# Two decoder layers on one core: the product a @ w_out of both MLPs as Strassen's seven block products

## What is computed

```python
def _mlp(h, w_in, w_out):
    a = jnp.square(jax.nn.relu(h @ w_in))     # h: 512 x 1024, w_in: 1024 x 4096
    return a @ w_out                          # w_out: 4096 x 1024

for l in range(DEPTH):                        # DEPTH = 2
    h = _rmsnorm(x, norm_mix[l])
    x = x + (_pool_mixer(...) if l < N_A else _diff_attn(...))
    x = x + _mlp(_rmsnorm(x, norm_mlp[l]), w_mlp_in[l], w_mlp_out[l])
    if l == N_A - 1:                          # after layer 0: shared keys and values
        kv = _rmsnorm(x, kv_norm) @ w_kv
```

## Time and profile before

| | |
|---|---|
| median of 3 runs | 1009.54 us (1009.34 to 1012.75) |
| the profiled execution's own time | 1010.91 us |
| its span, first to last instruction | 1009.1 us |
| PE busy (matmuls) | 990.1 us, 98% |
| DVE, ACT, POOL busy | 517.5, 407.1, 58.3 us |
| HBM read | 92.56 MB |
| MLP of layer 0, of layer 1 | about 32 to 385 us, about 652 to 1005 us |

### The profile page before, as it was taken

The page is one execution under the profiler, slowest core; times in us unless marked ns, Lnnn a source line. Parts: engine busy times, 40 slices in busy tenths (PEclk is TensorE's granted clock), DMA queues, the critical chain, the costliest instruction groups (busy, mean ns, idle before and its releaser), DMA issues.

```text
span 1009.1 us, 12484 instructions
## 1 busy us (share of the span) xinstructions
PE 990.1 (98%) x4663; PEld 816.4 (81%) x4663; DVE 517.5 (51%) x815; ACT 407.1 (40%) x586; POOL 58.3 (6%) x44
## 2 busy tenths in 40 slices
PE   8999999999999999899999999999999999999998
PEld 6888888888888887678888877888888888888886
DVE  5855422144442427888888885755441234444221
ACT  8643421223341315566666673534331113342110
POOL 2100000000000000222222230000000000000000
PEclk9999999999999999899999998999999999999999
DMA  7423223223323222232332222223323222423231
GB/s 241 121 84 108 100 85 124 84 83 91 117 83 119 91 62 63 66 90 84 85 86 86 73 83 84 84 84 91 116 84 123 87 84 87 121 83 105 83 105 42
DMA packets 82300, 95.15 MB, mean 94 GB/s; under 512 B 2690, under 2 KB 61107, under 8 KB 82267
## 3 DMA queue, kind: packets, MB, share of 16 engines
q1 hardware_dynamic: 80954, 89.95, 28.8%
q0 software_dynamic: 1312, 4.74, 1.6%
HBM read 92.56 MB, written 4.74 MB: 96 GB/s over the span
## 4 chain that ended last, share of the span: by engine, by line
PE 92%; DVE 4%; issue 1%; ACT 1%; DMA 1%; SPq 0%; DVEq 0%
PE bank L1087 29%; PE bank L1089 29%; PE bank L1088 29%; PE bank L1261 2%; PE bank L1271 1%; PE bank L1299 1%; PE bank L1216 1%; DMA work<-in_x_dram 1%; DVE work L914 1%; DVE neg_max L950 1%; DVE work L946 0%; PE bank L1185 0%; ACT work L635 0%; DVE a_low_buf L732 0%; DVE xT L830 0%
## 5 line engine op out<-in xcount | busy, mean ns | idle before, releaser
L723 DVE TENSOR_TENSOR w_low<-raw,w_high 128x2048 fp32r<-128x2048 f32 (+1 forms) x75 | 163.3, 2177 | 233.8 <-ACT w_high L463 233.7
L1087 PE MATMUL bank<-h_high_buf,w_high 128*128 128x512 f32 x640 | 252.9, 395 | 0.0
L1089 PE MATMUL bank<-h_high_buf,w_low 128*128 128x512 f32 x640 | 250.1, 391 | 0.0
L1088 PE MATMUL bank<-h_low_buf,w_high 128*128 128x512 f32 x640 | 249.9, 390 | 0.0
L463 ACT ACTIVATE w_high<-raw 128x2048 fp32r<-128x2048 f32 (+1 forms) x77 | 140.1, 1819 | 254.7 <-PE bank L1089 254.7
L1087 PE MATMUL bank<-a_high_buf,w_high 128*128 128x512 f32 x528 | 208.0, 394 | 4.1 <-DVE a_low_buf L732 4.0
L1089 PE MATMUL bank<-a_high_buf,w_low 128*128 128x512 f32 x528 | 206.6, 391 | 0.0
L1088 PE MATMUL bank<-a_low_buf,w_high 128*128 128x512 f32 x528 | 206.5, 391 | 0.0
L1087 PEld LDWEIGHTS bank<-h_high_buf,w_high 128*128 128x128 f32 x640 | 120.8, 189 | 27.4 <-issue 2.5
L1089 PEld LDWEIGHTS bank<-h_high_buf,w_low 128*128 128x128 f32 x640 | 120.6, 188 | 25.6
L1088 PEld LDWEIGHTS bank<-h_low_buf,w_high 128*128 128x128 f32 x640 | 120.8, 189 | 24.3
(11 more groups left out here) (133 smaller groups left out, 821.2 us busy)
## 6 DMA issues: line engine op xcount, KB each, us to landing
raw<-in_w_mlp_in_dram SPq DMA_DIRECT2D x32, 1024.0 KB, 5.5
raw<-in_w_mlp_out_dram SPq DMA_DIRECT2D x32, 1024.0 KB, 5.0
raw<-in_w_kv_dram SPq DMA_DIRECT2D x16, 512.0 KB, 4.0
raw<-in_w_q_dram SPq DMA_DIRECT2D x8, 512.0 KB, 5.3
raw<-in_w_o_dram SPq DMA_DIRECT2D x3, 1024.0 KB, 4.9
bias_by_distance<-bias_rows_by_distance POOLq DMA_DIRECT2D x8, 320.0 KB, 4.1
work<-in_x_dram SPq DMA_DIRECT2D x4, 512.0 KB, 5.1
work<-bias_by_distance POOLq DMA_DIRECT2D x8, 256.0 KB, 3.0
```

The costliest lines, as they stand in the source:

```text
L723: dve.tensor_tensor(w_low_buf[s][:, 0:cols], raw[s][:, 0:cols], f32(w_high_buf[s][:, 0:cols]), ALU.subtract)\
L1087: pe.matmul(acc, w_hi, m_hi, start=start, stop=False)
L1088: pe.matmul(acc, w_hi, m_lo, start=False, stop=False)
L1089: return pe.matmul(acc, w_lo, m_hi, start=False, stop=stop)
```

## The change

`a @ w_out` is computed per quarter of the 4096 rows of `w_out` (four pairs of chunks). In a quarter, `a` is split in two by tokens (2 x 256) and in two by rows, and `w_out` in two by rows and in two by columns (2 x 512). Seven products of blocks replace eight. Per pair of chunks ACT squares into a buffer `pre`, DVE forms four sums of blocks there (S1 to S4), and high and low parts of seven operands of 256 columns are made in one instruction each. A quarter's seven units follow in the order P1, P5, P2, P6, P3, P7, P4, each behind the fourth pair of its quarter and, but for the last quarter, behind the first pair of the next. A unit in layer 0 is 48 matmuls on 256 columns (weights: blocks of w_out), in layer 1 24 matmuls on 512 columns (weights: tokens). DVE adds or subtracts the product banks to the stream (`take`), 16 times a quarter; c21 is a second use of the banks of P7.

The sums of w_out blocks are made in `raw` buffers, of which there are four in the MLPs: T1 = B11 + B12 and T3 = B12 + B22 by a plain load and an adding transfer that POOL starts, T2 = T1 + B22 by DVE, T4 = T2 + B21 by an adding transfer. All loops of the MLPs are written out. The parts of the diff below are POOL's adding transfers, ACT's `split_out` and the end of its loop over the pairs (n = 2 to 15), DVE's `out_quarter`, and PE's `out_product`. The residual's transposes in layer 1 move behind the third and fourth pair. The inputs of the keys are prepared in the order of chunks 4 to 7, 0 to 3.

```diff
+            def add_blocks(l):
...
+                for q in range(NQ):
+                    pool.wait_ge(w_landed[0], landed[l, q, "t1"])
+                    pool.dma_start(tile3(mlp_raw[l][0], NPAIR), w_out_block(l, q, 0, 1), accum_op=ALU.add).then_inc(t1_landed, 16)
+                    pool.wait_ge(w_landed[1], landed[l, q, "t3"])
+                    pool.dma_start(tile3(mlp_raw[l][1], NPAIR), w_out_block(l, q, 1, 1), accum_op=ALU.add).then_inc(t3_landed, 16)
+                    pool.wait_ge(w_low, u_out(l, q, P6) + 1)
+                    pool.dma_start(tile3(mlp_raw[l][0], NPAIR), w_out_block(l, q, 1, 0), accum_op=ALU.add).then_inc(t4_landed, 16)
...
+            def split_out(l, q, p):
...
+                if p == P5:
+                    act.wait_ge(t1_landed, 16 * n)
+                elif p == P6:
+                    act.wait_ge(t2_ready, n)
+                elif p == P7:
+                    act.wait_ge(t3_landed, 16 * n)
+                elif p == P4:
+                    act.wait_ge(t4_landed, 16 * n)
+                else:
+                    act.wait_ge(w_landed[OUT_RAW[p]], landed[u])
+                act.wait_ge(w_used, u - 1)
+                act.activation(w_high_buf[u % 2][:, :], mlp_raw[l][OUT_RAW[p]], ACT.Copy).then_inc(w_high, 1)
...
+                    operands_high(l, n - 1)
...
+                    squares(l, n, 0)
...
+                    squares(l, n, 1)
+                    if n % 4 == 0:
+                        out_quarter(l, n // NPAIR - 1)
...
+            def out_quarter(l, q):
...
+                if q == NQ - 1:
+                    operand_sums(l, N_IN - 1)
+                split_out(l, q, P5)
+                if q == NQ - 1:
+                    operands_low(l, N_IN - 1, A12)
+                take_1(l, q, 0)
+                add_t2(l, q)
+                split_out(l, q, P2)
+                take_1(l, q, 1)
+                take_5(l, q, 0)
+                take_5(l, q, 1)
+                split_out(l, q, P6)
+                take_2(l, q, 0)
+                take_2(l, q, 1)
+                split_out(l, q, P3)
...
+                split_out(l, q, P4)
+                take_7(l, q, 0)
+                take_7(l, q, 1)
+                if q < NQ - 1:
+                    split_in(l, 4 * q + 5)
+                take_c21(l, q, 0)
+                take_c21(l, q, 1)
+                if l == 0 and q == NQ - 1:
+                    split_low(U_HEAD, 1)
+                    prep_kv(range(2))
+                take_4(l, q, 0)
+                if l == 0 and q == NQ - 1:
+                    prep_kv(range(2, 4))
+                take_4(l, q, 1)
...
+            def out_product(l, q, p, acc, fresh):
...
+                        if l == 0:
+                            for m in range(2):
+                                last = product(acc[t][:, m * TH:(m + 1) * TH], *column(u % 2, k * S + (2 * t + m) * P), a_hi, a_lo,
+                                               start and m == 0, stop and m == 1, not fresh)
                         else:
+                            tile, w = slice(t * P, (t + 1) * P), slice(k * S, (k + 1) * S)
+                            last = product(acc[t][:, :], a_hi[:, tile], a_lo[:, tile], w_high_buf[u % 2][:, w], w_low_buf[u % 2][:, w],
+                                           start, stop, not fresh)
```

More of the change, by code:

```diff
@@ L486, in norm_root_step, with prep_x @@
                    .then_inc(norm_rooted, 1)
-            def prep_x(h_base, x_base, dst, gain, chunks=range(KC)):
+            def prep_x(x_base, dst, gain, chunks=range(KC)):
                 for c in chunks:
@@ L491, in prep_x @@
                     input_high(dst[:, c, :], xT[:, c, :], params[:, gain + c:gain + c + 1])
[L493 to L504, removed]
@@ new lines, in squares, with operand_high @@
+            def squares(l, n, j):
+                cc = 2 * (N_IN * l + n) + j
+                if j == 0 and n >= 2:
+                    act.wait_ge(a_low, a_count(l, n - 2))
+                act.wait_ge(z_taken, cc + 1)
+                b = pre[n % 2]
+                act.activation(b[:, 0:8:7, :] if j == 0 else b[:, A12:A22 + 1, :], relu_buf[j].rearrange("p (h n) -> p h n", h=2), ACT.Square)\
+                   .then_inc(z_squared, 1)
+            def operand_high(l, n, first, last):
+                if n >= NPAIR:
+                    act.wait_ge(w_used, u_out(l, n // NPAIR - 1, P4) + 1)
+                act.activation(operand(a_high_flat, n, first, last), pre[n % 2][:, first:last, :].rearrange("p s n -> p (s n)"), ACT.Copy)\
+                   .then_inc(a_high, 1)
@@ L694, in _ @@
             o_high(6)
[L695 removed]
+            split_wo(U_WO + 2)
             o_copies(H - 1)
@@ new lines, in block, with take @@
+            def block(l, row, col, t):
+                if l == 0:
+                    return xT[:, 4 * col + 2 * t:4 * col + 2 * t + 2, row * TH:(row + 1) * TH]
+                return out_sb[:, 2 * row + t, col * S:(col + 1) * S]
+            def take(l, q, p, t, acc, row, col, op):
+                count = taken(l, q, p, t)
+                if t == 0:
+                    dve.wait_ge(tile_done, 7 * (NQ * l + q) + (P7 if p == "c21" else p) + 1)
+                else:
+                    dve.wait_ge(w_used, u_out(l, q, P7 if p == "c21" else p) + 1)
+                if count > 2:
+                    dve.wait_ge(tile_taken, count - 2)
+                x = block(l, row, col, t)
+                src = acc[t][:, :].rearrange("p (m n) -> p m n", m=2) if l == 0 else acc[t][:, :]
+                dve.tensor_tensor(x, x, src, op).then_inc(tile_taken, 1)
```

595 lines of the change are left out of this document (358 added, 237 removed).

## The result

| | before | after |
|---|---|---|
| median | 1010.75 us (4 runs) | 985.04 us (4 runs, 983.86 to 985.32) |
| span of the profiled execution | 1009.1 | 983.0 |
| its own time | 1010.91 | 984.77 |
| matmuls on PE | 4663 | 5143 |

The ratio is 0.9742 (0.972 to 0.9764). In a later series the changed kernel took 983.41 us (five runs) and the kernel before 1009.48 (nine), a ratio of 0.9742 (0.9721 to 0.9762). The forecast was 979.2, with 972 to 995 as its range; the first series misses it by 5.8 us and the later one by 4.2.

What follows compares the result with a forecast made beforehand. PE's back-to-back matmuls were taken to bound the kernel. Matmuls -38.7, waits +4.4 and transition +4.0 sum to -30.3 us: 1010.9 to 980.6 for the profiled execution, so a median of 979.2 us, range 972 to 995.

Steps and rivals of the forecast that it cites:

- 1344 x 0.117 = 157.2 us, so -16.9: Layer 0's w_out on PE: 1344 matmuls on 256 columns at 0.117 us each, against 174.1 us before.
- Layer 1's -21.8: Layer 1's w_out on PE: 672 instead of 768 matmuls on 512 columns, 152.3 us against 174.1.
- P5 and P2: PE's waits in w_out: P5 1.8 us in all, P2 in each layer's last quarter 2.6; sum +4.4 us.
- the covers that the forecast named: In the MLPs, transfers, takes and preparation beside the w_in pairs were to be hidden behind PE's work, at no cost.
- The transition: From layer 0 to the heads: low parts end 7.7 us behind P4's end; +4.0 us, bounds 2 and 6.
- took off 1.4 us: Last step of the sum: the profiled execution lies 1.4 us above the median, so 980.6 becomes 979.2.
- A: Rival: the adding transfer for T4 is late, each us over 13.3 costs 8 us; 997 at the bound; chance 0.16.
- its deadline: T4's adding transfer in each quarter: 12.7 us until ACT wants the result, 13.3 until PE stands.
- Its bound of 15.5: Upper bound in us for T4's landing: 4.1 for 320 KB scaled to 1 MB, plus four issues of 0.61.
- B's point of decision: Rival in layer 0's w_out: 256-column matmuls are slower, gain gone at a pitch of 0.1395 us; chance 0.07.
- C's reserve: Rival in w_out's cadence: DVE, with about 1 us reserve a unit, runs 0.4 late in 56 units, +22; chance 0.06.

Runs made afterwards that it cites:

- e1: The kernel before, with each w_out matmul of layer 0 issued as two on 256 columns and nothing else changed: 1020.9 us, ratio 1.0094.
- e8: The changed kernel, P5's high part ahead of the last squares (first three quarters) and T2 behind P2's low part (last quarter): 979.04 us, ratio 0.9689.
- e7: The changed kernel, with the keys' chunks 0 to 3 prepared ahead of the last square and the three sums behind layer 0: 984.22 us.
- e5: The changed kernel, with B21 added to T4 twice, one adding transfer behind the other, so T4 lands late: 1041.69 us, ratio 1.0288.
- e6: The changed kernel, with T4 made by DVE from the block SP has loaded instead of by an adding transfer: 984.28 us, ratio 0.9742.
- e9: The changed kernel, with the low parts of P6, P3 and P7 made twice in every quarter on DVE: 1001.64 us.
- c0: The changed kernel run again without an edit, as the measure for the runs beside it: 983.41 us.
- e2: The kernel before, with each w_out matmul of layer 0 issued as four on 128 columns: 1177.83 us.

## Why the prediction was right, and where it was off

**PE's matmuls: the term that was mis-sized.** The step "1344 x 0.117 = 157.2 us, so -16.9" took the pitch from a row of three matmuls, and starts in it are rounded to 0.01 us. Forty-two in a row, and e1 without the rest of the change, show 0.120: 161.3 us, so -12.8. That is +4.1 of the miss of 5.8 to the median of 985.04, and nearly all of the miss of 4.2 to the later median of 983.41. The value is the mean of the two rows that were given (0.117 and 0.123); taking one of them was the choice that failed, and the other would have missed by 4.0 the other way. Layer 1's -21.8 stands. The Trainium skill (TensorE: Matmul & The Clock Gate, Back-to-back issue gap) gives N/2.4 + 2.5 ns as the gap of an isolated matmul, and says of a stream of weight loads and matmuls that both set the spacing; the prediction left the second half out. In this stream what stands beside N/2.4 is 13 to 14 ns at 512 and at 256 columns alike (226.7 - 213.3, 120 - 106.7), and at 128 columns the pace is 112 ns where 53 + 13 would be 66.

**P5 and P2.** The forecast gave 0.13 four times, 0.31 four times and 1.3 twice, 4.4 in sum. e8 took away 0.09 three times, 0.44 three times, 0.91 and 1.18; with the two P5s of the last quarters, which e8 leaves and which are taken here as like the others, that makes 4.2. That the sums are so near is in part luck: P5 in layer 1 was taken 0.13 too low four times, and P2 0.4 and 0.1 too high. The places and the mechanism are as it said: the queue of relu, square, high part and low part at P5, and the low part of six operands and the T2 addition ahead of P2 where no later pair stands beside them.

**The stretches.** Layer 0's MLP: -12.8 from the matmuls, +0.4 and +0.9 for the waits, -11.5, as measured. Layer 1's: -21.8 + 1.8 + 1.2 = -18.8, measured -18.7. Both close on their own terms, so nothing is left that transfers, takes or the pairs of w_in would have to explain; the covers that the forecast named for them held.

**The transition.** Forecast +4.0, measured +3.8, by the steps named (low parts 7.7 us behind P4's end; 7.4 measured). e7 shows that it is the amount of DVE's work and not its order. The -1.0 in the attention was not forecast; no run was made for it, but the two traces put it down to shorter spells of half clock (1.1 us less lost), of which executions of one kernel differ as well.

**The start and the scatter.** The start's +1.7 us is in e1 as well and no step of the change. The forecast also took off 1.4 us because the profiled execution lay that far above the median of three runs; with a fourth run that median is 1010.75, and the profiled execution is 0.2 above it. So the miss of 5.8 is 4.1 for the pitch, 1.7 for the start and 1.4 for this step, less 1.0 in the attention, 0.4 at the end and 0.4 in the transition and the waits, to within 0.4. Against the later series (1009.48 before) the 1.4 was no error.

**The rivals.** A was priced too low, and its deadline was right: T4 lands in 8.1 to 9.1 us where 10 was taken and 13.7 are free, and e5, the only way to see it late, cost 57 us. Its 997 was too low: it counted the 18 us of waits alone. At its bound the waits would have been 2.2 us long; a wait of 2.5 us in the transition brought a spell of half clock in two executions of five (e6 and e9, not the kernel after, c0 or e8), so the price there would have been uncertain. Its bound of 15.5 also joined two different transfers: the 4.1 us are those of L440 with 320 KB, whose issue takes 0.53, and the 0.61 is L448's with 256 KB. An issue of 1 MB takes 1.28 us. The Trainium skill (SBUF — State Buffer, The "DVE blocks DMA" trap) had raised its chance; it ties the effect to DVE's 2-port operations, such as an fp32 copy, while DVE's work beside these issues is almost all TENSOR_TENSOR and SCALAR_TENSOR_TENSOR. 24 issues of POOL took 1273 to 1362 ns each beside a DVE that is 73% busy, so no run here shows DVE holding one back. B's point of decision was 0.1395, and with 0.120 for all 1344 layer 0's MLP closes. C's reserve of about 1 us a unit is what e9 shows.

## What to carry to other kernels

Take the pitch of a shape from the longest row of back-to-back starts the trace has, and where only three stand together, take the mean of several such rows: over 1344 matmuls 0.003 us are 4 us. Once PE's work per operand is halved, look for what is left of the gain in the two or three units whose preparation has something else in its queue (here the first product of a quarter and the second of the last), and reorder those; it gave a sixth more here. A wait of PE costs its row plus 0.26 us here, and behind all eight waits of 3 us or more that e5 put into the MLPs half clock followed, which cost as much as half of the waits again; so a transfer that must be on time deserves reserve, not thrift. Before a difference of one or two us between two traces is put down to a change, compare the spells of half clock in both.

## What the runs showed of the hardware that was not expected

- Matmuls that each load their weights start every 0.112 us on 128 columns (e2), every 0.120 on 256 (the kernel after, e1) and every 0.2267 on 512: under 256 columns there is next to nothing left to gain.
- An adding transfer of 1 MB landed in 8.1 to 9.2 us in the kernel after (T3 and T4; T1 in 8.3 to 11.6), against 5.8 in the median for a plain load from SP's queue beside it, and its issue held POOL for 1.28 us, against 0.53 for 320 KB (L440) and 0.61 for 256 KB (L448).
- Behind each of e5's eight waits of 3.0 to 7.4 us, PE ran for 3.4 to 6.1 us at half clock although its operands were there; behind e9's 21 waits of up to 1.3 us it did not. Elsewhere it varies from execution to execution: the two waits of 2.3 and 1.4 to 1.8 us in the attention had a spell behind them in all ten traces (2.8 to 6.0 us of work), the one of 3.3 to 3.4 us in seven of the ten (not in e2, e7 and e9), the transition's 2.5 us in two of five. Three short waits close together had one in e7 (1.8, 1.1 and 0.4 us) and in e5 (1.0, 1.0 and 0.4).
- The start, where PE has several waits of 0.2 to 1.8 us, had a spell of half clock in seven of ten traces and none in three (the kernel before, e5, e9); it cost 1.6 to 1.7 us.
